# One-core decoder block, mixture of experts: ranks dealt over the row slots, a 16-column projection on four column tiles, and other runs made narrow

## What is computed

```python
x = x + hybrid_mixer(rms_norm(x, g_mix), ...)            # attention heads beside a gated linear attention (GLA)
x = x + memory_cross_attention(rms_norm(x, g_cross), ...)
x = x + moe_ffn(rms_norm(x, g_ffn), ...)
return rms_norm(x, g_final)

# in the mixer; w_in has 3088 columns, ga are its last 16:
proj = h @ w_in                                          # ... ga = proj[:, 3072:3088]
log_a = log_sigmoid(ga @ w_alpha2 + b_alpha) / 16        # w_alpha2 is 16 x 256

# moe_ffn: 32 experts, each token goes to the 4 with the largest logits
logits = t @ w_router + b_router
u = xb @ w_up[e] + b_up[e]                               # 1024 -> 2048, for the tokens of expert e
act = min(u[:, :1024], 7) * sigmoid(1.702 * ...) * (clip(u[:, 1024:], -7, 7) + 1)
y = act @ w_down[e] + b_down[e]                          # 1024 -> 1024, times the gate, added to the token
```

## Time and profile before

| | |
|---|---|
| runs | 1596.36, 1598.2, 1591.67 us; median 1596.36 us |
| profiled execution, own time | 1600.94 us |
| its span | 1599.2 us |
| TensorE busy | 1509.5 us, 94% of the span |
| VectorE, ScalarE, GpSimd busy | 518.5, 247.5, 180.8 us |
| DMA | 468.42 MB; 400 to 416 GB/s in nearly every fortieth of the span after 640 us |
| mean granted clock of TensorE | 0.985 of full speed |

### The profile page before, as it was taken

How to read it: one execution, slowest core, us unless ns; L and a number is a source line. 1 busy time by engine, 2 the same in 40 slices (tenths; PEclk the granted TensorE clock), 3 DMA queues, 4 the chain that set the end, 5 groups by cost and what they waited for, 6 DMA issues and landing times.

```text
span 1599.2 us, 28460 instructions
## 1 busy us (share of the span) xinstructions
PE 1509.5 (94%) x11025; PEld 626.2 (39%) x11025; DVE 518.5 (32%) x1356; ACT 247.5 (15%) x556; POOL 180.8 (11%) x185
## 2 busy tenths in 40 slices
PE   7999999999999799999999999999999999999994
PEld 3444466554554434333333333423324242333331
DVE  3214335440213445233222422333224232332223
ACT  3113333311212101011000110010101110010002
POOL 1000000060001011201111011110111102011101
PEclk9999999999999899999999999999999999999997
DMA  6211023042012899999999999999999999999994
GB/s 240 98 60 53 1 105 106 1 139 84 35 53 79 346 384 389 402 411 407 408 410 400 416 410 409 405 409 415 412 408 410 415 414 408 410 415 411 412 384 145
DMA packets 87647, 468.42 MB, mean 293 GB/s; under 512 B 12562, under 2 KB 12614, under 8 KB 38288
## 3 DMA queue, kind: packets, MB, share of 16 engines
q1 hardware_dynamic: 75960, 443.68, 68.1%
q0 software_dynamic: 11504, 23.08, 5.5%
q10 hardware_dynamic: 72, 0.02, 0.0%
HBM read 454.68 MB, written 17.43 MB: 295 GB/s over the span
## 4 chain that ended last, share of the span: by engine, by line
PE 63%; DMA 31%; DVE 3%; issue 1%; ACT 1%; ACTq 0%; POOL 0%; SPq 0%; DVEq 0%; POOLq 0%
DMA arena<-in_w_up 27%; PE bank L780 24%; PE bank L839 13%; PE bank L861 8%; PE bank L894 6%; PE bank L904 3%; DMA ring<-in_w_up 2%; DMA arena<-h_rows,arena 1%; PE bank L852 1%; PE bank L1057 1%; PE bank L1040 1%; PE bank L1083 1%; PE bank L928 1%; PE bank L811 1%; PE bank L984 1%
## 5 line engine op out<-in xcount | busy, mean ns | idle before, releaser
L839 PE MATMUL bank<-ring,arena 128*32 128x512 f32 x2768 | 306.0, 593 | 8.9 <-DMA ring<-in_w_up 8.9
L780 PE MATMUL bank<-ring,actT 128*128 128x512 f32 x448 | 201.4, 606 | 0.1
L861 PE MATMUL bank<-arena 128*32 128x512 f32 x1312 | 163.4, 599 | 18.6 <-DMA arena<-in_w_up 17.7
L839 PEld LDWEIGHTS bank<-ring,arena 128*32 128x32 f32 x2768 | 88.4, 110 | 218.1 <-issue 195.4
L1752 DVE TENSOR_SCALAR tokA<-bank 64x512 f32<-64x512 f32 x64 | 43.7, 683 | 395.0 <-PE bank L839 387.7
L839 PE MATMUL bank<-actT,arena 128*32 128x512 f32 x1312 | 147.2, 594 | 0.0
L674 POOL DMA_INDIRECT arena<-h_rows,arena x31 | 33.3, 1074 | 838.3 <-DVE arena L1723 812.1
L894 PE MATMUL bank<-arena 128*32 128x512 f32 x1024 | 125.2, 593 | 2.1 <-DMA arena<-in_w_down 2.1
L894 PE MATMUL bank<-ring,arena 128*32 128x512 f32 x992 | 120.7, 593 | 5.7 <-DMA ring<-in_w_down 5.5
L780 PEld LDWEIGHTS bank<-ring,actT 128*128 128x128 f32 x448 | 85.4, 195 | 100.6 <-issue 99.8
L1334 ACT ACTIVATE tokA<-tokA 128x512 f32<-128x512 f32 x32 | 20.2, 630 | 492.9 <-DVE tokA L1752 492.9
(11 more groups left out here) (347 smaller groups left out, 1471.2 us busy)
## 6 DMA issues: line engine op xcount, KB each, us to landing
ring<-in_w_up SPq DMA_DIRECT2D x130, 1024.0 KB
arena<-in_w_up SPq DMA_DIRECT2D x64, 1024.0 KB
arena<-in_w_down SPq DMA_DIRECT2D x64, 1024.0 KB
actT<-in_w_up SPq DMA_DIRECT2D x62, 1024.0 KB, 25.6
ring<-in_w_down SPq DMA_DIRECT2D x62, 1024.0 KB
ring<-in_w_in SPq DMA_DIRECT2D x12, 1024.0 KB
ring<-in_w_ck SPq DMA_DIRECT2D x4, 1024.0 KB
ring<-in_w_out SPq DMA_DIRECT2D x4, 1024.0 KB
```

The lines of the kernel that those rows point to most:

```text
L780: mm = pe.matmul(o, lhsT, rhs, start=(k == 0), stop=(k == KT - 1))
L839: mm = pe.matmul(bank[g][32 * t:32 * t + 32, :], lhsT, w[:, 512 * t:512 * t + 512], start=False, stop=(k == KT - 1))
L861: mm = pe.matmul(bank[g][32 * t:32 * t + 32, :], lhsT, moe_slot[(o + k) % MOE_RING][:, 512 * t:512 * t + 512], start=False, stop=False)
```

## The change

It has three parts. (1) The slots are renumbered: within each block of 32 slots the rank is dealt so that four neighbouring slots hold ranks a, a + 8, a + 16, a + 24 (in B backwards, from 7 - a), and A's two blocks of 32 ranks now stand one behind the other in each 64 partitions, with the two halves of the row 64 partitions apart. The layouts that follow from it (`xTA`, the order of column tiles in `down`, `rowA_c`) go along; `slot_no` is written by eight iotas in place of three, `pick0` by two operations for each block of tokens in place of one. (2) `ga` uses the four column tiles in turn with 32 columns, of which 16 are zeros, so that eight products leave four partial sums in the 128 partitions of the bank; `w_al` is loaded four times, 32 partitions apart, with zeros between, and `gate_z` adds the four up. GpSimd zeroes both tiles first, and SP waits for that (`ga_zero`) ahead of the load of `w_ga`. (3) Narrow runs are 2, 3, 7, 10, .. 31: again eleven narrow and 21 wide, but run 31 is narrow. The loops of three cover runs 6 to 29.

```diff
-        self.wide = n != 2 and (n < 3 or n % 3 != 0)
+        self.wide = n not in (2, 3) and (n < 7 or n % 3 != 1)
...
-        w_ga = aT[:, 0, 0:16 * KT].rearrange("p (k n) -> p k n", k=KT)
-        w_al = sb("w_al", [16, 256])
+        w_ga = aT[:, 0, 0:32 * KT].rearrange("p (k n) -> p k n", k=KT)
+        w_al = aT[:, 1, 0:256]
...
-        gaT = pbuf[0:16, 0, :]
+        gaT = pbuf[:, 0, :]
...
-        xTA = carve(KT * WIDE, "p (i g h n) -> p i g h n", i=KT // 2, g=2, h=2)
+        xTA = carve(KT * WIDE, "p (i h g n) -> p i h g n", i=KT // 2, g=2, h=2)
...
-        LOOP_FROM, LOOP_TURNS = 4, (NE - 8) // 3
+        LOOP_FROM, LOOP_TURNS = 6, (NE - 8) // 3
...
-                sp_.dma_start(w_ga[:, :, :], A["w_in"][0].rearrange("(k p) n -> p k n", p=P)[:, :, 3072:3088]).then_inc(small_in, 16)
-                sp_.dma_start(w_al[:, :], A["w_alpha2"][0]).then_inc(small_in, 16)
+                sp_.wait_ge(ga_zero, 2)
+                sp_.dma_start(w_ga[:, :, 0:16], A["w_in"][0].rearrange("(k p) n -> p k n", p=P)[:, :, 3072:3088]).then_inc(small_in, 16)
+                for t in range(4):
+                    sp_.dma_start(w_al[32 * t:32 * t + 16, :], A["w_alpha2"][0]).then_inc(small_in, 16)
...
+            g.memset(w_ga[:, :, :], 0.0).then_inc(ga_zero, 1)
+            g.memset(w_al[:, :], 0.0).then_inc(ga_zero, 1)
...
-            made(from_partition(rowA_c, 32, 2.0 * OOB + 1))
-            made(from_partition(rowA_c, 64, 2.0 * OOB))
-            const(from_partition(rowA_c, 96, 2.0 * OOB + 1))
+            const(from_partition(rowA_c, 64, 2.0 * OOB + 1))
...
-            for half in range(2):
-                g.iota(slot_no[:, :, 64 * half:64 * half + 64], pattern=[[W, BLOCKS], [0, 2], [1, NARROW]], base=NARROW * half,
+            for q in range(8):
+                fours = slot_no[:, :, 32 * q:32 * q + 32].rearrange("p j (a b) -> p j a b", b=4)
+                g.iota(fours, pattern=[[W, BLOCKS], [1 if q < 4 else -1, 8], [8, 4]], base=NARROW * (q % 2) if q < 4 else WIDE + 7,
                        channel_multiplier=0, allow_small_or_imprecise_dtypes=True).then_inc(iota_ready, 1)
-            g.iota(slot_no[:, :, P:2 * P], pattern=[[W, BLOCKS], [0, 4], [1, NARROW]], base=WIDE, channel_multiplier=0,
-                   allow_small_or_imprecise_dtypes=True).then_inc(iota_ready, 1)
...
-            g.memset(rank_of_run[:, 2:3], 19.0).then_inc(sort_consts, 1)
-            turns_ = rank_of_run[:, 3:NE + 1].rearrange("p (t u) -> p t u", u=3)
+            for n, rank in ((2, 19.0), (3, 20.0), (4, 18.0)):
+                g.memset(rank_of_run[:, n:n + 1], rank).then_inc(sort_consts, 1)
+            turns_ = rank_of_run[:, 5:NE].rearrange("p (t u) -> p t u", u=3)
...
-                                rr = 64 * g + 32 * t
+                                rr = 64 * t + 32 * g
...
                     for k in range(KT):
-                        mm = pe.matmul(ps(s)[0:16, :], w_ga[:, k, :], actT[:, k, :], start=(k == 0), stop=(k == KT - 1))
+                        r = 32 * (k % 4)
+                        mm = pe.matmul(ps(s)[r:r + 32, :], w_ga[:, k, :], actT[:, k, :], start=(k < 4), stop=(k >= 4))
...
-                    slots = slot_no[:, 0, :].rearrange("p (q n) -> p q n", n=WIDE)[:, 0:3, 0:NARROW]
-                    v.tensor_scalar(pick0[:, b, :].rearrange("p (q n) -> p q n", q=3), slots, slot_rank[:, b, 0:1], None,
+                    v.tensor_scalar(pick0[:, b, 0:WIDE], slot_no[:, 0, 0:WIDE], slot_rank[:, b, 0:1], None, ALU.is_equal)
+                    v.tensor_scalar(pick0[:, b, WIDE:W], slot_no[:, 0, P:P + NARROW], slot_rank[:, b, 0:1], None,
                                     ALU.is_equal).then_inc(pick_ready, 1)
```

More of the change, by code:

```diff
@@ L357, in decoder_block @@
         consts_ready = sem("consts_ready")
-        gcol_ready = sem("gcol_ready")
+        gcol_ready, ga_zero = sem("gcol_ready"), sem("ga_zero")
         rstd_ready, xn_ready = sem("rstd_ready"), sem("xn_ready")
@@ L653, in _ @@
             g.memset(rank_of_run[:, 1:2], NE - 1.0).then_inc(sort_consts, 1)
-            g.memset(rank_of_run[:, 2:3], 19.0).then_inc(sort_consts, 1)
-            turns_ = rank_of_run[:, 3:NE + 1].rearrange("p (t u) -> p t u", u=3)
-            g.iota(turns_[:, :, 0:1], pattern=[[1, 10], [0, 1]], base=20, channel_multiplier=0,
+            for n, rank in ((2, 19.0), (3, 20.0), (4, 18.0)):
+                g.memset(rank_of_run[:, n:n + 1], rank).then_inc(sort_consts, 1)
+            turns_ = rank_of_run[:, 5:NE].rearrange("p (t u) -> p t u", u=3)
+            g.iota(turns_[:, :, 0:2], pattern=[[2, 9], [1, 2]], base=0, channel_multiplier=0,
                    allow_small_or_imprecise_dtypes=True).then_inc(sort_consts, 1)
-            g.iota(turns_[:, :, 1:3], pattern=[[2, 10], [1, 2]], base=0, channel_multiplier=0,
+            g.iota(turns_[:, :, 2:3], pattern=[[1, 9], [0, 1]], base=21, channel_multiplier=0,
                    allow_small_or_imprecise_dtypes=True).then_inc(sort_consts, 1)
-            g.wait_ge(iota_ready, 3)
+            g.wait_ge(iota_ready, 8)
             g.memset(xgA, 0.0).then_inc(xg_zero, 1)
@@ L836, in up_pair @@
                     for g in range(3 if r.wide else 2):
-                        lhsT = xTA[:, k % 4, g, k // 4, :] if g < 2 else xTB[:, k % 4, k // 4, :]
+                        lhsT = xTA[:, k % 4, k // 4, g, :] if g < 2 else xTB[:, k % 4, k // 4, :]
                         for t in range(4):
@@ L858, in up_first @@
                             expert_chunk_in(pe, q, o + k)
-                        lhsT = xTA[:, k, g, 0, :] if g < 2 else xTB[:, k, 0, :]
+                        lhsT = xTA[:, k, 0, g, :] if g < 2 else xTB[:, k, 0, :]
                         for t in range(4):
@@ L879, in down @@
                         c0 = 2 * FF + 512 * t
-                        pe.matmul(bank[3][64 * g + 32 * t:64 * g + 32 * t + 32, :], sel_down[:, 0:NARROW], bias_bf[:, c0:c0 + 512],
+                        pe.matmul(bank[3][64 * t + 32 * g:64 * t + 32 * g + 32, :], sel_down[:, 0:NARROW], bias_bf[:, c0:c0 + 512],
                                   start=True, stop=False)
@@ L950, in _ @@
                 elif kind == "ga":
-                    pe.wait_ge(small_in, 16 * 8)
+                    pe.wait_ge(small_in, 16 * 11)
                     pe.wait_ge(actT_lo["mix"], NB)
@@ L1207, in _ @@
                     x3 = bank[3][:, 0:4 * W].rearrange("p (i n) -> p i n", i=4)
[L1208 removed]
+                    a.activation(xTA[:, :, 0, :, :], x3[:, :, 0:WIDE].rearrange("p i (g n) -> p i g n", g=2), ACT.Copy)
                     a.activation(xTB[:, :, 0, :], x3[:, :, WIDE:W], ACT.Copy).then_inc(xTA_ready, 1)
@@ L1254, in _ @@
                     ready(a, s)
-                    act_evac(a, a.activation(gaT, ps(s)[0:16, :], ACT.Copy), s, ga_ready)
+                    act_evac(a, a.activation(gaT, ps(s)[:, :], ACT.Copy), s, ga_ready)
                 elif kind == "gla_decay":
@@ L1328, in rows_out_A @@
                 a.wait_ge(xgT_done, r.times(1, 1))
-                a.activation(xTA.rearrange("p i g h n -> p (i g h n)"), bank[5][:, :], ACT.Copy).then_inc(xTA_ready, 1)
+                a.activation(xTA.rearrange("p i h g n -> p (i h g n)"), bank[5][:, :], ACT.Copy).then_inc(xTA_ready, 1)
             def gates(r):
@@ L1450, in _ @@
                 elif kind == "lam":
-                    v.wait_ge(small_in, 16 * 8)
+                    v.wait_ge(small_in, 16 * 11)
                     for q in range(2):
@@ L1680, in _ @@
                     x4 = bank[4][:, 0:4 * W].rearrange("p (i n) -> p i n", i=4)
-                    v.tensor_copy(xTA[:, :, :, 1, :], x4[:, :, 0:WIDE].rearrange("p i (g n) -> p i g n", g=2))
+                    v.tensor_copy(xTA[:, :, 1, :, :], x4[:, :, 0:WIDE].rearrange("p i (g n) -> p i g n", g=2))
                     v.tensor_copy(xTB[:, :, 1, :], x4[:, :, WIDE:W]).then_inc(xTB_ready, 1)
@@ L1796, in _ @@
             rows_of(Run(1))
-            v.wait_ge(sort_consts, 6)
+            v.wait_ge(sort_consts, 8)
             own(v.scalar_tensor_tensor(out=key, in0=count_f[:, :], scalar=float(NE), in1=tie[:, :], op0=ALU.mult, op1=ALU.add))
```

3 lines of the change are left out of this document (1 added, 2 removed).

## The result

| | before | changed |
|---|---|---|
| median of the runs taken together | 1596.44 us (8 runs) | 1587.3 us (8 runs, 1585.67 to 1589.37) |
| ratio, 95% interval | | 0.9947 [0.9936, 0.9959] |
| span of the profiled execution | 1599.2 us | 1586.2 us |

The ratio is 8.5 us of 1596.4. The two profiled executions differ by 13.0 us in their spans, but the one of before lay 4.5 us above its median and the one of after 0.7 us, so what a single profile says of a stage holds to some 4 us.

What follows compares the result with a forecast made beforehand. TensorE bounds the front; DMA bounds the experts' stage, with TensorE 4% behind. The terms -5.1 + 0.4 - 9.5 - 2.3 = -16.5 us, against the 1596.4 us median, give 1579.9 us; range 1573 to 1591 us.

Steps and rivals of the forecast that it cites:

- rival (a): Experts' DMA: the deal evens nothing, unevenness from a slow engine or instruction fetches; 1589.4 us, chance 0.12.
- the main mechanism: Experts' stage: dealing ranks evens the DMA engines' row work, so the last weights land earlier; 9.5 us less.
- ga, -5.1: Front: eight products on four column tiles take 1.92 us instead of 7.04, all on TensorE's path.
- 0.6 us for each of two drains: Front, ga: extra gain by the skill's rule, 1.2 us together; the forecast went by rows showing no such gap.
- The small costs, +0.4: Front: second pick0 operation costs 0.2 us for each of two token blocks; extra loads and iotas taken as nothing.
- The engines, -9.5: Experts' DMA: dealt ranks even the engines' row work; 9.5 us less, between 0 and 10.6 us.
- partly filled blocks: Experts' row moves: half-filled blocks make engines uneven, a lag of up to 20 us against 10.6 seen.
- the staircase: End of the weights: DMA shares falling 0.88, 0.60, 0.33, 0.32, 0.04; forecast to become 1, then 0 within one or two windows.
- The end, -2.3: Last run narrow: A's last product ends 2.0 us after the last landing instead of 4.3 us.
- the bound of 0 to 1 us: End: shortening from A's last product to the reading back once B's scatter falls away; taken as 0.

Runs made afterwards that it cites:

- e1: Kernel before with only the 16-column projection ga put on four column tiles: ratio 0.9962, 6.1 us less.
- e3: Kernel before with only the deal of ranks over the slots and the layouts that follow: ratio 0.9995, 0.8 us less.
- e4: Changed kernel without the deal, ranks in order as before: ratio 0.9943 to the kernel before, median 1586.94 us.
- e5: Changed kernel with the bound of every gather and scatter set to 0, so nearly no row is moved: 1545.66 us in one execution.
- e12: Changed kernel, but SP loads a chunk only when four more have been used, eight of twelve ring slots in use: ratio 1.0012, median 1597.8 us.
- e2: Kernel before with only the other choice of narrow runs, so the last run is narrow: ratio 0.9986, 2.2 us less.
- e10: Changed kernel itself, unchanged, timed again on one chip beside the changed kernel without the deal: ratio 0.9941, median 1585.86 us.

## Why the prediction was right in sign and too large

Predicted were 1579.9 us, with 1573 to 1591, and faster at 0.87. It came to 1587.3 us: inside the range, faster by 8.5 us where 16.5 had been summed. The miss is one term, the largest. The time is nearer to the 1589.4 us of rival (a), that the deal evens nothing, at a chance of 0.12. That the result still lies below the 1588.4 us from which on the prediction spoke of faster is luck as far as the main mechanism goes: it does so by 1.1 us, with that mechanism giving nothing that shows.

**ga, -5.1: right.** The records go from 7.04 to 1.92 us as in the sum, and e1 measured 6.1 us, an interval that holds 5.1. By the rule of the Trainium skill's "TensorEngine Tiling (Array Packing)", section Key Properties, that a change of tiling mode drains the array, and the prediction's estimate of 0.6 us for each of two drains, 3.9 us should have come. The timeline shows no drain of that size: the next group starts at 75.80 us, when 73.95 + 1.92 are over, within 0.1 us, as it did before. e1's interval ends at 4.2 us, just above the 3.9; a drain of under 0.1 us isn't excluded.

**The small costs, +0.4: not seen by themselves.** VectorE's second `pick0` operation is there, and e3 and e4 bound it together with the iotas: the deal with all its instructions costs nothing that shows. The loads of `w_al` and the wait on `ga_zero` are in e1, which gave 6.1 us with them: they cost nothing that shows, though its interval would hide 1 us.

**The engines, -9.5: this step failed.** It measured 0.8 us alone, and 0.6 in the mean of three comparisons. Two inferences went into it. The first was that the unevenness comes from partly filled blocks, since the size fitted (up to 20 us against 10.6 seen). It does so only in part: the landings show that the deal halves the drift, but it does so by holding back the engine that ran ahead, and the slowest engine is as late as before. The size was no evidence, and it was worked out too large as well. 512 tokens go to 4 experts each in two halves, which makes 4096 rows and not 4416; and q0 keeps 1.6% of the span when no row moves (e5), so that some 4% of it, about 64 us and not 88, are rows. The second inference was that the staircase, summed up, is what evening gives, with 10.6 us as the upper bound. e12 and the landings show that the staircase is a stock that fills up to the depth of the ring, here by chunk 180 of 384 with the ranks in order, and then grows no more. It can be as long as ever after half of the drift has been taken away, and shows nothing of what the slowest engine costs.

By the rule that I had cited beside it, the Trainium skill's "DMA: Bandwidth & Descriptors", section The descriptor swizzle (an engine takes four neighbouring partitions and the four 32 further on), the whole 10.6 us should have come. The measured 0.8 us say that evening by this rule doesn't give the gain. That the engine ahead is gone after the deal agrees with engines that take neighbouring slots, but no run tells how gathers and scatters are shared out.

The prediction had written that it would be wrong on the mechanism if the staircase stayed and the time fell nevertheless. That is what the windows show.

**The end, -2.3: right.** A ends 2.1 us after the last landing (2.0 predicted). e2 measured 2.2 us, and its profile shows 2.3. The scatter of B is gone from the last run, and from the end of the last product to the reading back it is 1569.59 - 1563.58 = 6.0 us where it was 7.0: the bound of 0 to 1 us held, at its upper end in this one profile.

**What keeps the engines apart is known in part.** The order of ranks was one source, of an engine ahead (the landings of nine profiles). Rows are a second, beyond their order: without B's the distance grows more slowly (11.0 us at chunk 240, for 16.2 to 17.8) and the slowest engine gains 12.6 us from chunk 36 on (925.2 us for e10's 937.8), about the 11.9 us of the stage. The fetches of instructions are a third: each holds up one engine by 1.5 to 1.7 us. That is a source of the kind that rival (a) had named; in e5 it is there and hidden from the time, since TensorE is the limit. No run took the fetches away, so what they cost in time isn't measured.

## What to carry to other kernels

When the shares of the DMA engines fall in steps at the end of a stream, don't sum the steps into a gain: shorten or lengthen the ring once and see whether the steps go along, and follow the last report of the loads from chunk to chunk: only what makes the slowest engine faster is worth time. An unevenness whose cause is only inferred from its size gets its own experiment, here the order of ranks alone, before anything is built on it. Small products with few columns are worth putting on the four column tiles wherever TensorE is the limit, and a stream of weights should end on its lightest run; both came as computed, within their intervals.

## What the runs showed that I had not expected

**The front's length differs by 9 us between executions, with TensorE's clock.** The start of the first expert's product was at 534.77 us in one profile of kernels with the same front, and at 544.05 in another (eleven profiles; without ga's part, three profiles gave 545.64 to 548.76). The granted clock tells where. In e4, which had 534.77 us, and then in the changed kernel, which had 541.53:

```profile
170.00:180.00 10.00, 8.27 (x27) 4.15 (x27) 2.09 (x7) 4.12 (x15) 0.00 (x0) 1.00 0.01 2
520.00:530.00 10.00, 4.47 (x46) 3.55 (x45) 5.05 (x24) 1.18 (x4) 0.00 (x0) 0.77 1.01 413
530.00:540.00 10.00, 10.00 (x80) 4.93 (x78) 5.56 (x26) 1.83 (x3) 0.00 (x0) 0.71 1.01 422
```

```profile
170.00:180.00 10.00, 7.44 (x19) 3.60 (x20) 3.30 (x10) 4.93 (x16) 0.00 (x0) 0.83 0.01 2
520.00:530.00 10.00, 7.46 (x61) 6.79 (x61) 4.14 (x16) 0.97 (x3) 1.05 (x2) 0.83 1.01 401
530.00:540.00 10.00, 6.80 (x42) 6.39 (x46) 2.45 (x14) 0.21 (x1) 0.00 (x0) 0.58 1.01 424
```

A mean of 0.58 is a stretch mostly at the lower of the two levels, 1.2 GHz. It comes where TensorE had been waiting for VectorE and ScalarE in pieces of 1 to 2 us, between the router and the first expert. Both kernels have these waits. One group of 32 records with `pick0` (L1086 of the changed kernel) took 3.79 us in e4 and 5.42 us in the changed kernel. Where exactly the dips fall differs from one execution to the next, and it makes a part of 7.2 us in the front look like more than ga's 5.1. So the stage from the first expert's product on was the better measure of the deal.

**Rows are dear.** They are 16.44 of 468 MB, 3.5% of the bytes, but without them the kernel is 41.6 us faster. Alone, the scatters, which add, cost 32.4 us and the gathers 21.2, together more than 41.6, since TensorE is the limit when both are gone. The queue's share falls from 5.6% to 2.9% without the first and to 4.4% without the second, for 8.35 and 8.09 MB, so that a byte of a scatter takes about twice the time of a gathered one.

**Depth of the ring is worth time where the experts start.** Four slots less cost 10 us, 8 of them between 560 and 580 us (see above). Afterwards it is 407 GB/s from 600 to 1500 us in place of 409 (e10, the changed kernel's second profile), and TensorE's waits for `w_up` are 28.5 us in place of 24.7, but from chunk 36 on the last landings lose only 1.2 us more. Whether more than twelve slots would give something wasn't tried.
